# A two-block transformer on one core: the shared-key attention in rounds of one group and two heads, and the sums of the layer norms on GpSimd

## The reference

```python
def dilated_group(q, k, v, slopes, window, dilation):      # 16 heads of 64; cut
    scores = jnp.einsum("bpnqhd,bpnkhd->bpnhqk", qb, kw) * (1.0 / math.sqrt(dh))
    bias = -slopes[:, None, None] * (dist * dilation).astype(jnp.float32)[None]
    scores = jnp.where(valid[:, None], scores + bias, NEG_INF)
    ...

def dilated_attention(x, k, v, w_q, w_o):
    q = (x @ w_q).reshape(bsz, s, N_GROUPS, N_HEADS, HEAD_DIM)      # 3 groups of queries, one set of keys and values
    slopes = alibi_slopes(N_HEADS)                                  # 2 ** (-8 (h + 1) / 16)
    for g, (window, dilation) in enumerate(((128, 1), (512, 4), (2048, 16))):
        o, l = dilated_group(q[:, :, g], k, v, slopes, window, dilation)
        outs.append(o); lses.append(l)
    wts = jax.nn.softmax(jnp.stack(lses, axis=0), axis=0)
    out = jnp.sum(wts[..., None] * jnp.stack(outs, axis=0), axis=0)
    return out.reshape(bsz, s, N_HEADS * HEAD_DIM) @ w_o

def layer_norm(x, g, b):
    mu = jnp.mean(xf, axis=-1, keepdims=True)
    xc = xf - mu
    var = jnp.mean(xc * xc, axis=-1, keepdims=True)
    return xc * lax.rsqrt(var + LN_EPS) * g + b
```

## Time and profile before

| | |
|---|---|
| Time, median of 3 runs | 1805.95 us (1804.25 to 1807.08) |
| The profiled execution | 1804.63 us, span 1802.8 us, mean granted TensorE clock 0.988 |
| Busy: TensorE (PE), its weight loads (PEld) | 1764.2 us (98%), 1600.3 us (89%) |
| Busy: VectorE (DVE), ScalarE (ACT), GpSimd (POOL) | 1290.2 us (72%), 977.2 us (54%), 0.2 us |
| DMA | 290.77 MB, 161 GB/s over the span |

### The profile page before, as it was taken

The page is one execution under the profiler, slowest core; times in us unless marked ns, Lnnn a source line. Parts: engine busy times, 40 slices in busy tenths (PEclk is TensorE's granted clock), DMA queues, the critical chain, the costliest instruction groups (busy, mean ns, idle before and its releaser), DMA issues.

```text
span 1802.8 us, 33249 instructions
## 1 busy us (share of the span) xinstructions
PE 1764.2 (98%) x11768; PEld 1600.3 (89%) x11768; DVE 1290.2 (72%) x2099; ACT 977.2 (54%) x1708; POOL 0.2 (0%) x4
## 2 busy tenths in 40 slices
PE   9999999999999999999999998999999999999998
PEld 7888998888899888888788887889999998898887
DVE  6777789777665776778787766868655568787765
ACT  5564695656355554455465544565534355565543
POOL 0000000000000000000000000000000000000000
PEclk9999999999999999999999999999999999999999
DMA  7665465456545566422356663334455533346562
GB/s 223 189 200 192 127 198 170 149 187 206 180 142 176 189 194 201 138 89 100 104 202 187 196 196 111 117 112 135 140 175 193 181 118 118 112 134 198 186 204 88
DMA packets 76637, 290.77 MB, mean 161 GB/s; under 512 B 9344, under 2 KB 11648, under 8 KB 76544
## 3 DMA queue, kind: packets, MB, share of 16 engines
q1 hardware_dynamic: 76544, 289.50, 50.5%
HBM read 288.42 MB, written 1.05 MB: 161 GB/s over the span
## 4 chain that ended last, share of the span: by engine, by line
PE 91%; DVE 5%; ACT 2%; issue 1%; DMA 0%; SPq 0%; ACTq 0%; DVEq 0%
PE psum L500 33%; PE psum L501 17%; PE psum L492 11%; PE psum L494 11%; PE psum L493 11%; DVE wlo L1508 1%; PE psum L632 1%; PE psum L738 1%; PE psum L627 1%; DVE r L1680 1%; PE psum L579 1%; PE psum L737 1%; ACT whi L1043 1%; PE psum L860 1%; PE psum L867 1%
## 5 line engine op out<-in xcount | busy, mean ns | idle before, releaser
L1508 DVE TENSOR_TENSOR wlo<-raw,whi 128x1024 fp32r<-128x1024 f32 (+3 forms) x496 | 644.8, 1309 | 245.9 <-ACT whi L1043 245.1
L500 PE MATMUL psum<-x_split,whi 128*128 128x512 f32 x1760 | 618.4, 395 | 3.6 <-DVE x_split L1543 2.1
L1043 ACT ACTIVATE whi<-raw 128x1024 fp32r<-128x1024 f32 (+3 forms) x496 | 548.7, 1119 | 40.4 <-PE psum L494 21.5
L501 PE MATMUL psum<-x_split,wlo 128*128 128x256 f32 x1760 | 494.6, 281 | 0.0
L500 PEld LDWEIGHTS psum<-x_split,whi 128*128 128x128 f32 x1760 | 331.3, 188 | 81.8 <-DVE x_split L1543 2.5
L492 PE MATMUL psum<-x_split,whi 128*128 128x272 f32 (+1 forms) x1184 | 346.3, 293 | 4.6 <-DVE x_split L1716 3.4
L494 PE MATMUL psum<-x_split,wlo 128*128 128x272 f32 (+1 forms) x1184 | 338.6, 286 | 0.0
L493 PE MATMUL psum<-x_split,whi 128*128 128x272 f32 (+1 forms) x1184 | 337.7, 285 | 0.0
L501 PEld LDWEIGHTS psum<-x_split,wlo 128*128 128x128 f32 x1760 | 332.2, 189 | 0.0
L500 PE MATMUL psum<-h_split,whi 128*128 128x512 f32 x770 | 272.2, 397 | 0.0
L492 PEld LDWEIGHTS psum<-x_split,whi 128*128 128x128 f32 x1184 | 223.4, 189 | 14.9 <-issue 9.1
(11 more groups left out here) (231 smaller groups left out, 1769.8 us busy)
## 6 DMA issues: line engine op xcount, KB each, us to landing
raw<-w_in SPq DMA_DIRECT2D x264, 512.0 KB, 3.5
raw<-w_out SPq DMA_DIRECT2D x96, 704.0 KB, 4.4
raw<-w_mix SPq DMA_DIRECT2D x44, 512.0 KB, 3.6
raw<-w_rg SPq DMA_DIRECT2D x25, 512.0 KB, 4.1
raw<-w_q SPq DMA_DIRECT2D x24, 512.0 KB, 3.7
raw<-w_mixo SPq DMA_DIRECT2D x16, 576.0 KB, 3.7
raw<-w_kv SPq DMA_DIRECT2D x16, 512.0 KB, 3.7
raw<-w_rg_out SPq DMA_DIRECT2D x8, 640.0 KB, 3.9
```

What stands on the lines that cost most here:

```text
L500: nc.tensor.matmul(ps[:, bank, :], whi[slot][:, w], split, start=start, stop=False)
L501: return nc.tensor.matmul(part(bank, 0), wlo[slot][:, w], split[:, 0], start=False, stop=stop)
L1043: nc.scalar.activation(whi[slot][:, 0:cols], raw[slot][:, 0:cols], ACT.Copy).then_inc(w_hi_done, count)
L1508: V.tensor_tensor(wlo[slot][:, 0:cols], raw[slot][:, 0:cols], f(whi[slot][:, 0:cols]), ALU.subtract).then_inc(w_lo_done, 1)
```

## The change

The attention is done in 24 rounds, one for each q tile n, that is for one group of both heads of a pair. The scores of the two heads stand side by side in two banks (2 and 3 for even rounds, 4 and 5 for odd ones), and their matmuls alternate between partitions 0 to 63 and 64 to 127. The bias and the minimum of the negated scores come from one VectorE instruction (`tensor_tensor_reduce`) for each head and block of query tokens; to make that possible the slope is divided out of the queries (a scale per partition in the eviction of the q tile). A second buffer for the exponentials of a pair lies in a free part of `h_split`. The normalisation is in the second of the two additions of `sum_groups`. The values of both heads alternate as well. Transposes go to bank 6, the outputs of all pairs to bank 7. The order on each engine is by q tile, and at the end output tiles 0, 1 and 2 of stage `o` are begun with 7, 7 and 5 contracted tiles.

The sums of the norms are made by GpSimd: 12 additions for each of the ten norms (tiles 0 to 6 and their squares), into the same `sums`; VectorE's additions and its clearing of `sums` are gone.

```diff
             first = isinstance(i, int) and i == 0
-            todo = [k for k in range(tiles) if not (begun and first and j < 2 and k in begun)]
+            todo = [k for k in range(tiles) if not (begun and first and k in begun[j])]
...
-            def scores(a):
-                hp, rows = a // 2, slice(HD * (a % 2), HD * (a % 2 + 1))
-                pe.wait_ge(acc_free, st.u0 + GROUPS * (hp + 1))
-                if a:
-                    pe.wait_ge(biased, a)
-                for g in range(GROUPS):
-                    nc.tensor.matmul(ps[:, 2 + g, 0:P], qT[rows, hp % 2, g, 0:P], kT[rows, hp, 0:P], start=True, stop=True)
-                    last = nc.tensor.matmul(ps[:, 2 + g, P:SCORES], qT[rows, hp % 2, g, P:SEQ], kT[rows, hp, :],
-                                            start=True, stop=True)
-                last.then_inc(scored, 1)
+            def scores(n):
+                hp, g = n // GROUPS, n % GROUPS
+                pe.wait_ge(acc_free, st.u0 + n + 1)
+                if n >= 2:
+                    pe.wait_ge(round_biased, n - 1)
+                for queries, keys in ((slice(0, P), slice(0, P)), (slice(P, SEQ), slice(0, SEQ))):
+                    for e in range(2):
+                        rows = slice(HD * e, HD * (e + 1))
+                        cols = TOKEN_TILES[queries.start // P]
+                        last = nc.tensor.matmul(ps[:, round_bank(n, e), cols], qT[rows, hp % 2, g, queries], kT[rows, hp, keys],
+                                                start=True, stop=True)
+                last.then_inc(round_scored, 1)
...
+            def values(hp):
+                pe.wait_ge(pT_copied, 2 * hp + 2)
+                if hp:
+                    pe.wait_ge(at_ready, hp)
+                for t in range(2):
+                    for e in range(2):
+                        a = 2 * hp + e
+                        ins = nc.tensor.matmul(ps[HD * e:HD * (e + 1), 7, P * t:SEQ], v_tok[:, t, HD * a:HD * (a + 1)],
+                                               pT[:, e, SEQ * t:SEQ * t + SEQ - P * t], start=t == 0, stop=t == 1,
+                                               skip_group_check=True)
...
+            begun = (range(PAIRS - 1), range(PAIRS - 1), range(PAIRS - 3), ())
+            def begin_output(j, tiles):
+                pe.wait_ge(at_ready, tiles[-1] + 1)
+                for k in tiles:
+                    begin(so, j, k)
+            for s in range(Q_TILES + 6):
+                if s < Q_TILES:
+                    query(s)
+                if s == Q_TILES:
+                    begin_output(0, range(0, 3))
+                if s == Q_TILES + 1:
+                    begin_output(0, range(3, 6))
+                if s == Q_TILES + 2:
+                    begin_output(1, range(0, 3))
+                if s == Q_TILES + 3:
+                    begin_output(1, range(3, 6))
+                if s == Q_TILES + 4:
+                    for j in range(2):
+                        begin_output(j, range(6, 7))
+                if s == Q_TILES + 5:
+                    begin_output(2, range(0, 5))
+                if 1 <= s <= Q_TILES:
+                    scores(s - 1)
+                if s >= 6 and s % 3 == 0:
+                    transposed(2 * (s // 3 - 2))
+                if s >= 6 and s % 3 == 1:
+                    transposed(2 * (s // 3 - 2) + 1)
+                if s >= 6 and s % 3 == 2:
+                    values(s // 3 - 2)
...
+    @block.gpsimd
+    def _(pool):
+        own = [0]
+        def add(row, t, a, b):
+            own[0] += 1
+            if own[0] > 2:
+                pool.wait_ge(pool_step, own[0] - 2)
+            nc.gpsimd.tensor_tensor(sums[:, row, t], a, b, ALU.add).then_inc(pool_step, 1)
+        for ns, name in enumerate(norm_stages):
+            st, T = by_name[name], tokens[name]
+            t = slice(tok0(T), TOK)
+            n = norm_no[name]
+            if n:
+                pool.wait_ge(stat_done, n)
+            pool.wait_ge(shifted, ns + 1)
+            for m in range(1, KD - 1):
+                pool.wait_ge(acc_free, st.u0 + m + 1)
+                add(0, t, r[:, 0, t] if m == 1 else sums[:, 0, t], r[:, m, t])
+                pool.wait_ge(sq_done, KD * n + m + 1)
+                add(1, t, sq[:, 0, t] if m == 1 else sums[:, 1, t], sq[:, m, t])
+            pool.wait_ge(pool_step, own[0])
+            pool.sem_inc(sums_done, 1)
...
+            for s in range(Q_TILES + 7):
+                if s < Q_TILES:
+                    round_ahead(st, s // SLOTS, s % SLOTS)
+                if s >= 8 and s % 3 == 2:
+                    copy_transposed(2 * ((s - 8) // 3) + 1)
+                if s >= 9 and s % 3 == 0:
+                    round_output((s - 9) // 3)
+                if s >= 7 and s % 3 == 1:
+                    copy_transposed(2 * ((s - 7) // 3))
+                if 5 <= s < Q_TILES + 4 and s % 3 == 2:
+                    exps(2 * ((s - 5) // 3))
+                if 6 <= s < Q_TILES + 4 and s % 3 == 0:
+                    exps(2 * ((s - 6) // 3) + 1)
+                if s in (Q_TILES + 3, Q_TILES + 5):
+                    next_chunk(by_name["o"], 0, (s - Q_TILES) // 2 - 1)
+                if s < Q_TILES:
+                    query_tile(s)
...
-            if last:
-                link(add_square(2))
-                add_square(1).then_inc(sums_done, 1)
-            elif not first and not (isinstance(i, int) and m == 1):
-                add_square(2)
...
+            def bias_max(n):
+                hp, g = n // GROUPS, n % GROUPS
+                b = hp % 2
+                dve.wait_ge(round_scored, n + 1)
+                if hp >= 2:
+                    dve.wait_ge(pT_done, 2 * hp - 2)
+                for e in range(2):
+                    for t, cols in enumerate(TOKEN_TILES):
+                        ins = V.tensor_tensor_reduce(s_pair[b][:, e, g, cols], ps[:, round_bank(n, e), cols], dist[:, g, cols],
+                                                     -head_slope(2 * hp + e), 3e38, ALU.add, ALU.min, nmax_g[:, b, e, t, g:g + 1])
+                ins.then_inc(round_biased, 1)
+                if g == GROUPS - 1:
+                    dve.wait_ge(round_biased, n + 1)
+                    V.tensor_reduce(nmax[:, b, :, :], nmax_g[:, b, :, :, :], AX.X, ALU.min).then_inc(nmax_done, 1)
             def sum_groups(a):
...
+                V.reciprocal(rden[:, b, e, :], den[:, b, e, :])
+                link(V.tensor_tensor(s[:, e, 1, :], s[:, e, 1, :], s[:, e, 2, :], ALU.add))
+                for t, cols in enumerate(TOKEN_TILES):
+                    ins = V.tensor_tensor_reduce(s[:, e, 0, cols], s[:, e, 0, cols], s[:, e, 1, cols], rden[:, b, e, t:t + 1], 0.0,
+                                                 ALU.add, ALU.add, total[:, b, e, t:t + 1])
+                ins.then_inc(probs_ready, 1)
...
+            for s in range(Q_TILES + 7):
+                if s < Q_TILES:
+                    rest(s)
+                if 2 <= s < Q_TILES + 2:
+                    bias_max(s - 2)
+                if 5 <= s < Q_TILES + 4 and s % 3 == 2:
+                    sum_groups(2 * ((s - 5) // 3))
+                if 6 <= s < Q_TILES + 4 and s % 3 == 0:
+                    sum_groups(2 * ((s - 6) // 3) + 1)
+                if s >= 9 and s % 3 == 0:
+                    rest_of_output((s - 9) // 3)
+                if s in (Q_TILES + 3, Q_TILES + 5):
+                    rest_of_chunk(*ahead(by_name["o"], 0, (s - Q_TILES) // 2 - 1))
```

More of the change, by code:

```diff
@@ L748, in transposed @@
                 for n in range(SCORES // P):
-                    last = nc.tensor.transpose(ps[:, 5, n * P:(n + 1) * P], s_at[:, a % 2, 0, n * P:(n + 1) * P], ident)
+                    last = nc.tensor.transpose(ps[:, 6, n * P:(n + 1) * P], s_pair[hp % 2][:, e, 0, n * P:(n + 1) * P], ident)
                 last.then_inc(pT_done, 1)
[L752 to L778, removed]
-                if hp >= 2:
-                    transposed(behind)
-                if hp < PAIRS:
-                    query(3 * hp + 1)
-                if hp == PAIRS:
-                    for k in early[:3]:
-                        begin(so, 1, k)
-                if hp >= 2:
-                    values(behind)
-                if 1 <= hp <= PAIRS:
-                    transposed(a)
-                if hp < PAIRS:
-                    query(3 * hp + 2)
-                if hp == PAIRS:
-                    for k in early[3:]:
-                        begin(so, 1, k)
-                if 1 <= hp <= PAIRS:
-                    values(a)
@@ L799, in hybrid @@
+            steps(pe, so.chunks, lambda i, j: from_h(so, i, j, KD, ready=lambda k: pe.wait_ge(at_ready, k + 1), begun=begun))
         def hybrid(l):
@@ L1629, in less_shift @@
                 return V.scalar_tensor_tensor(tile, acc(7, T), float(-KD), tile, ALU.mult, ALU.add).then_inc(signal, 1)
-            def add_square(late):
-                dve.wait_ge(sq_done, i + (KD * norm_no[st.name] + j - late + 1))
```

(13 more changed lines are left out.)

148 lines of the change are left out of this document (54 added, 94 removed).

## The result

The changed kernel took 1787.2 us (median of 4 runs, 1784.4 to 1788.8), the kernel before 1805.3 on the same chip (1804.3 to 1807.1): a ratio of 0.9897, 95% interval 0.9882 to 0.9912. It is faster by 18 us; forecast were 1788.0, in a range of 1780 to 1797. On another chip, beside three of the experiments, the ratio was 0.9892 (0.9877 to 0.9907). There one of the changed kernel's five executions ran at a granted clock of 0.64 (2467.8 us) and is not in the ratio.

What follows compares the result with a forecast made beforehand. TensorE was taken to bound the kernel, with other engines setting the end of the attention's tail. Gains of 14.2 (q loop), 2.0 (tail) and 0.3 (norms) sum to 16.5 us, giving 1788 us; range 1780 to 1794, or 1797 with two rivals.

Steps and rivals of the forecast that it cites:

- The q loop: Attention's 21 q tiles: with two heads side by side, 93.0 us against 107.2, so 14.2 us less.
- I add two thirds, 0.15 and 0.10: Attention rounds: the second head adds 0.15 us to scores and 0.10 to values, two thirds of the hybrid layers' excess.
- the lower bound given: Attention's q loop: if the second head adds nothing to a block, the gain is 17.8 us.
- The excess of 0.22: Hybrid layers' scores: a second alternating head adds 0.22 us to a block of three shapes.
- VectorE keeps up: Attention's q loop: VectorE needs 11.2 us of a pair's 13.5, some 80 to 85%, so no waits.
- The wait in the loop: Attention's q loop, rival, 7%: full VectorE steps hold TensorE back, a pair takes 14.4 us, 6.3 less gain, 1796.
- The tail: Behind the last q tile: 34.6 us against 39.7, 5.1 less; after 3.1 lost to the clock, 2.0 us of gain.
- the loss by the clock: Behind the tail's idle time: the same drop in granted clock as before, 3.1 us lost.
- The norms: Norms' sums moved to GpSimd: 0.3 us gained in stage `o`, nothing in the other nine; bounds +0.7 to -0.1.
- I take 0.8. Then `sums_done` comes at about 911.9: Norm of `o`: a GpSimd addition takes 0.8 us, so the sums are ready 0.5 us ahead of 912.43.
- the first rival: Narrow norms: GpSimd and VectorE shut each other out, up to 1.2 us late in each of four, 4.9 us, 1793; 13%.
- signs of being wrong: Queued score matmuls, TensorE waiting on VectorE's bias, longer `sums_done` waits in narrow norms, or 1.22 us remainders stretched beside GpSimd.

Runs made afterwards that it cites:

- experiment 6: Experiment 2's kernel with all matmuls of the first head, then all of the second, in each round's scores and values; 1788.2 us, ratio 0.9902.
- experiment 7: Experiment 2's kernel with the second head's scores moved behind the step's three transposes in 13 rounds; 1798.7 us, ratio 0.9962.
- experiment 8: Experiment 2's kernel, but GpSimd makes the sums of the norm `o` alone; 1784.6 us, ratio 0.9883.
- experiment 4: Experiment 2's kernel plus as many GpSimd additions of the same size at the same places, into a buffer nobody reads; 1801.7 us, ratio 0.9983.
- experiment 2: The changed kernel's attention alone, with the norms' sums on VectorE as in the kernel before; 1787.5 us, ratio 0.9898.
- experiment 1: The changed kernel itself, run again on one chip beside the runs that take it apart; median 1786.3 us, ratio 0.9892.
- experiment 3: Experiment 2's kernel, but GpSimd makes the sums of the six wide norms behind the feed-forward stages; 1787.5 us, ratio 0.9897.
- experiment 9: Experiment 8's kernel with the work behind the last q tile reordered on VectorE, ScalarE and TensorE; 1780.7 us, ratio 0.9862.
- experiment 10: Experiment 2's kernel with experiment 9's reordered tail, all norms' sums on VectorE; 1783.5 us, ratio 0.9883.
- experiment 5: The kernel before with only the norms' sums moved to GpSimd, its attention unchanged; 1807.1 us, ratio 1.0015.

## Why the prediction was right, and where its terms were not

The total was right to 1 us, with three terms off. In the two profiled executions, by the starts of corresponding matmuls, the attention from the norm of `out2` to the last product of `o` is 20.9 us shorter (forecast 16.2); the rest of the program gave back 5, where 0.3 more of gain was forecast. That 4.7 too little and 5.4 too much all but cancel is luck.

**The q loop: 17.6 us, forecast 14.2.** The mechanism was right, the step "I add two thirds, 0.15 and 0.10" was mis-sized: the measured excess is 0.01 us for scores (0.86 against 0.85 for one head alone) and 0.00 for values. That was the lower bound given, 17.8. The excess of 0.22 was read from the hybrid layers, at other shapes; why it is larger there no run shows. The pair took 13.0 us, forecast 13.5, bound 13.0. That the heads alternate in the program was not needed (experiment 6); that they stand together is (experiment 7).

**VectorE keeps up.** Forecast 11.2 us of a pair of 13.5, or 80 to 85%; measured 66.4 of 88.8 us, 75%, and TensorE without idle time. The forecast added up durations, and VectorE's instructions overlap at their ends: the remainder of 886.66 ends at 888.33, and L1670 starts at 888.25. The wait in the loop didn't come.

**The tail: 3.3 us (39.66 - 36.33), forecast 2.0.** Idle time was 4.5 us (36.33 - 31.79) against 4.7 forecast, but not all at the places named. The waits for pair 6 (1.57, forecast 2.2), for the last output (0.97, forecast 1.1) and for the transposes of head 14 (0.44, forecast 1.4) came; 1.23 us for the output of pair 5, at 860.75, were not in the forecast, and 0.34 are the shift's. What was too high was the loss by the clock: 3.1 forecast, and the row of 868 to 872 us at 0.58 makes it 1.7. Experiment 8, with the same idle time, had none. The drop is no fixed price of a pause.

**The norms: a loss, forecast 0.3 of gain.** The step that failed is "I take 0.8. Then `sums_done` comes at about 911.9": an addition takes 0.73 us alone, as assumed, but 1.71 when it meets a weight remainder. So the first rival was true as a mechanism, together with the forecast, and cheaper than its 4.9 us: 0.65 us more of gap in each of `rg_out`, `mixo0` and `mixo1`, and 0.6 in `o`. Two of the prediction's own signs of being wrong came true here: the wait for `sums_done` grew, and the remainders are stretched. By the next stage's first product 0.5, 0.8, 0.0 and 0.4 us are left, 1.7 in all. The 0.0 of `mixo1` is the clock's doing: behind it the kernel before had 0.58 from 1601 to 1605 us, the changed kernel 1.00. Against experiment 8, where VectorE makes these sums and the clock is whole as well, `mixo1` costs 0.5 too (7.86 against 7.33 us from last to next product). The Trainium skill's rule (SBUF — State Buffer, SBUF: two separate sides), that the two engines exclude each other at the memory port, fits the two timelines and experiment 4. No run varied the number of SBUF inputs alone; that L1670, with one of them, keeps its 0.42 us beside GpSimd agrees with the rule. The Trainium skill's figure for GpSimd's addition, an estimate of 0.83 us (GPSIMD Engine Reference, Performance versus the Vector engine), is near the 0.73 of an undisturbed one.

**What the forecast didn't see: the halves depend on each other.** I priced the sums against the gap of the kernel before. It was 1.14 us at `o`. With the faster attention and VectorE's sums it is 3.33; GpSimd brings it to 1.74. So at `o` the sums' move earns its place: from the last product to the next stage's first it is 11.88 us in experiment 2 and 8.63 in the change. Part of these 3.25 us is the clock, low for less time in the change's profile. In experiment 8, with GpSimd at `o` and the clock low for as long as in experiment 2 (0.57 from 892 to 900 us, there from 893 to 901), it is 9.97 us, so some 1.9 us are GpSimd's. In `rg_out`, `mixo0` and `mixo1` it loses 0.5 to 0.8 us each. Alone it costs 2.8 us. Over the whole kernel the two roughly cancel, by experiments 1 and 2.

**What is left.** Some 3 us of the difference between the stages' sum and the total lie in the last hybrid layer and the two feed-forward stages around it, of which 1.4 to 1.7 is the low clock at 1476 to 1484 us, with VectorE and TensorE busy for as long as before. The profiles of experiments 3, 6, 8, 9 and 10 show it too, those of experiments 2, 4, 5 and 7 and of the kernel before don't. Neither half of the change decides it, and I did not find what does.

## What to carry to other kernels

The scores of two heads, on different halves of the array's rows, cost here no more than those of one, in either order of the program, as long as no transpose on all rows stood between them; so did the values, which go to different halves of the output partitions. Put such matmuls together, and don't pay for a fine order. Before moving work to GpSimd, look for long VectorE instructions with two inputs in SBUF on the same stretch: if the stage has slack the move costs nothing and gives nothing, and in a tight one every meeting lengthens both. It pays only where VectorE sets the pace and is left with less per tile than before, as in `o`. When two edits meet in one stage, price the second against the stage as the first leaves it.

## What the runs showed of the hardware

- Four passes of one head's scores take 0.85 us, and eight passes of two heads 0.86, whether the program alternates the heads or not. The values take 0.80 for one head and 0.80 for two.
- In stage `o` GpSimd's addition of two 128x256 fp32 tensors takes 0.73 us undisturbed, and 1.71 to 1.73 when it meets a 1.22 us instruction of VectorE; that one becomes 1.32 to 1.77. Over the changed kernel the 85 additions that overlap a weight remainder by less than 0.1 us take 0.73 to 0.78 us, the 35 others up to 1.92. GpSimd's means:

```profile
L1059 POOL TENSOR_TENSOR sums<-sums,r 128x256 f32<-128x256 f32 x40 | 44.8, 1120 | 163.8 <-DVE r L1690 163.8
L1059 POOL TENSOR_TENSOR sums<-sums,sq 128x256 f32<-128x256 f32 x40 | 32.5, 812 | 0.1
```

- Unused work on an idle engine isn't free: 120 additions by GpSimd that nobody reads cost 14 us.
- Behind 4.5 us of idle time in the tail the granted clock was 0.58 over 4 us in one kernel and 1.00 in another with the same order of work (experiment 8). TensorE's clock behind short pauses isn't a fixed price; some 1.5 us at the start of the program differ in the same way (0.86 in the change and 1.00 in experiment 2, from 4 to 16 us).
